# Feed-forward activation transposed by block turns and sixteen small DMAs instead of by TensorE

## The reference

```
for l in range(DEPTH):                      # DEPTH = 2
    ...
    x = x + (mixed @ w_o[l])
    h = rms_norm(x, ffn_norm[l])
    gate, up = split(h @ w_gate_up[l], 2)   # each 256 x 5632
    x = x + ((silu(gate) * up) @ w_down[l])
```

## Time and profile before

| | us |
|---|---|
| median of 3 runs | 2346.24 (2345.91 to 2346.59) |
| the profiled execution | 2346.4 |
| its span, first to last instruction | 2344.1 |
| PE busy | 2320.8 (99%) |
| DVE busy | 1323.1 (56%) |
| ACT busy | 1102.6 (47%) |
| POOL busy | 36.0 (2%) |

### The profile page before, as it was taken

The page is one execution under the profiler, slowest core; times in us unless marked ns, Lnnn a source line. Parts: engine busy times, 40 slices in busy tenths (PEclk is TensorE's granted clock), DMA queues, the critical chain, the costliest instruction groups (busy, mean ns, idle before and its releaser), DMA issues.

```text
span 2344.1 us, 33374 instructions
## 1 busy us (share of the span) xinstructions
PE 2320.8 (99%) x13481; PEld 1922.3 (82%) x13481; DVE 1323.1 (56%) x1420; ACT 1102.6 (47%) x1362; POOL 36.0 (2%) x50
## 2 busy tenths in 40 slices
PE   8999999999999999999999999999999999999999
PEld 7888688888888888888888886888888888888887
DVE  5686676545454445445557857665554444454454
ACT  6554755544443344444445547464444433444433
POOL 0000100000000000000000001000000000000000
PEclk9999999999999999999999999999999999999999
DMA  7453305555555555555554533145555555555553
GB/s 300 166 185 121 131 21 185 189 184 195 187 189 190 190 195 197 182 195 180 194 184 153 196 110 108 39 167 189 184 196 187 189 190 190 195 196 183 194 182 141
DMA packets 59518, 407.03 MB, mean 174 GB/s; under 512 B 6608, under 2 KB 6704, under 8 KB 13200
## 3 DMA queue, kind: packets, MB, share of 16 engines
q1 hardware_dynamic: 58720, 401.66, 48.2%
q0 software_dynamic: 688, 3.78, 0.5%
HBM read 403.32 MB, written 2.10 MB: 173 GB/s over the span
## 4 chain that ended last, share of the span: by engine, by line
PE 95%; DVE 2%; ACT 1%; issue 0%; DMA 0%; SPq 0%; DVEq 0%; ACTq 0%
PE psum L1466 28%; PE psum L1468 28%; PE psum L1467 28%; PE psum L1660 2%; PE psum L1755 2%; PE psum L1909 1%; PE psum L1996 1%; PE psum L1561 1%; PE psum L1500 1%; PE psum L1710 1%; PE psum L1716 0%; DMA x<-x_in_dram 0%; PE psum L1764 0%; PE psum L1569 0%; ACT arena L644 0%
## 5 line engine op out<-in xcount | busy, mean ns | idle before, releaser
L881 DVE TENSOR_TENSOR w_lo<-raw,w_hi 128x1024 fp32r<-128x1024 f32 (+2 forms) x752 | 901.3, 1205 | 844.6 <-ACT w_hi L442 838.1
L442 ACT ACTIVATE w_hi<-raw 128x1024 fp32r<-128x1024 f32 (+2 forms) x752 | 782.0, 1044 | 1071.6 <-PE psum L1468 1070.1
L1466 PE MATMUL psum<-w_hi,hT_hi 128*128 128x512 f32 (+2 forms) x2128 | 821.6, 386 | 3.7 <-DVE w_lo L881 3.7
L1468 PE MATMUL psum<-w_hi,hT_lo 128*128 128x512 f32 (+2 forms) x2128 | 816.5, 384 | 0.0
L1467 PE MATMUL psum<-w_lo,hT_hi 128*128 128x512 f32 (+2 forms) x2128 | 816.3, 384 | 0.0
L1466 PEld LDWEIGHTS psum<-w_hi,hT_hi 128*128 128x128 f32 x2128 | 399.7, 188 | 82.3 <-DVE w_lo L881 2.4
L1468 PEld LDWEIGHTS psum<-w_hi,hT_lo 128*128 128x128 f32 x2128 | 399.6, 188 | 78.2
L1467 PEld LDWEIGHTS psum<-w_lo,hT_hi 128*128 128x128 f32 x2128 | 399.8, 188 | 76.7
L1466 PE MATMUL psum<-w_hi,act_hi 128*128 128x512 f32 x872 | 340.4, 390 | 0.0
L1468 PE MATMUL psum<-w_hi,act_lo 128*128 128x512 f32 x872 | 339.4, 389 | 0.0
L1467 PE MATMUL psum<-w_lo,act_hi 128*128 128x512 f32 x872 | 339.3, 389 | 0.0
(11 more groups left out here) (315 smaller groups left out, 1133.1 us busy)
## 6 DMA issues: line engine op xcount, KB each, us to landing
raw<-stream_dram SPq DMA_DIRECT2D x360, 1024.0 KB, 4.8
raw<-stream_dram SPq DMA_DIRECT2D x16, 512.0 KB, 3.8
raw<-stream_dram SPq DMA_DIRECT2D x8, 768.0 KB, 4.3
raw<-stream_dram SPq DMA_DIRECT2D x8, 640.0 KB, 3.9
x<-x_in_dram SPq DMA_DIRECT2D x4, 512.0 KB, 9.3
lor<-lora_dram POOLq DMA_DIRECT2D x2, 832.0 KB, 10.4
con<-consts_dram POOLq DMA_DIRECT2D x1, 1648.0 KB, 11.2
out_dram<-x SPq DMA_DIRECT2D x3, 512.0 KB, 7.1
```

What stands on the lines that cost most here:

```text
L442: nc.scalar.activation(w_hi[:, q % HALF_RING, 0:2 * w], raw[:, j % 4, hf * 2 * w:(hf + 1) * 2 * w], ACT.Copy).then_inc(hi_done, 1)
L881: tt(w_lo[:, q % HALF_RING, 0:2 * w], raw[:, j % 4, hf * 2 * w:(hf + 1) * 2 * w], w_hi[:, q % HALF_RING, 0:2 * w].bitcast(F32), SUB).then_ ...
L1466: mm(o, a_hi, w_hi[:, r, cols], start=(k == 0), stop=False)
L1468: last = mm(o, a_lo, w_hi[:, r, cols], start=False, stop=(k == n_k - 1))
```

## The change

PE's turn is gone, with its waits. In its place:

- DVE writes act_row so that the two token tiles alternate in runs of 32 columns, and then turns all 32x32 blocks of the 128x1024 tile with one transpose instruction into `act_blocks` (half of `gain`). It waits for the end of that before it goes on.
- A full transpose also needs the blocks moved between the four groups of 32 partitions. POOL waits for each pair's block turn and issues sixteen DMAs of 32 partitions x 256 columns (32 KB), from `act_blocks` to `act_moved` (the other half of `gain`): one for each pair of source and target group, 22 x 16 = 352 in all.
- ACT and DVE read `act_moved` where they read PSUM; ACT waits for all sixteen DMAs.

```
+        act_blocks = gain[:, 0:2 * CH]
+        act_moved = gain[:, 2 * CH:4 * CH]
+        n_moves = (P // 32) ** 2
...
+                for i in range(sum(PAIRS) * l, sum(PAIRS) * (l + 1)):
+                    pool.wait_ge(S("act_blocks_turned"), i + 1)
+                    for q in range(P // 32):
+                        for b in range(P // 32):
+                            pool.dma_start(act_moved[32 * q:32 * q + 32, 256 * b:256 * b + 256],
+                                           act_blocks[32 * b:32 * b + 32, 256 * q:256 * q + 256]).then_inc(
+                                               S("act_moved"), 16)
...
                     def turned_hi(i, p0):
-                        act.wait_ge(S("act_turned"), i + (p0 + 1))
-                        dst = act_hi[:, bass.ds(i * 4, 4), :] if not isinstance(i, int) else act_hi[:, 4 * i:4 * i + 4, :]
-                        nc.scalar.activation(dst, bank(4, 2).rearrange("p (k t) -> p k t", k=4),
+                        act.wait_ge(S("act_moved"), i * (16 * n_moves) + 16 * n_moves * (p0 + 1))
+                        k = bass.ds(i * 4, 4) if not isinstance(i, int) else slice(4 * i, 4 * i + 4)
+                        nc.scalar.activation(act_hi[:, k, :].rearrange("p k (t b e) -> p (k t) b e", t=TT, e=32),
+                                             act_moved.rearrange("p (b n e) -> p n b e", n=8, e=32),
                                              ACT.Copy).then_inc(S("act_hi_ready"), 1)
...
-                        if not isinstance(i, int) or i + p0 > 0:
-                            dve.wait_ge(S("act_turned"), i + p0)
-                        stt(act_row[:, 0, :], psum[:, 2, :], rstd[:, 0:1], silu[:, 0, :], MUL, MUL)
-                        stt(act_row[:, 1, :], psum[:, 3, :], rstd[:, 1:2], silu[:, 1, :], MUL, MUL).then_inc(acc_free[1], 1)
+                        for t in range(TT):
+                            last = stt(act_row.rearrange("p a b -> p (a b)").rearrange(
+                                "p (n t r) -> p t n r", n=16, t=TT)[:, t],
+                                psum[:, 2 + t, :].rearrange("p (n r) -> p n r", n=16), rstd[:, t:t + 1],
+                                silu[:, t, :].rearrange("p (n r) -> p n r", n=16), MUL, MUL)
+                        last.then_inc(acc_free[1], 1)
                         dve.wait_ge(acc_free[1], i + (gate_base + 2))
                         dve.sem_inc(S("act_row_ready"), 1)
+                        nc.vector.transpose(act_blocks.rearrange("p (q k n) -> p k q n", q=4, k=4),
+                                            act_row.rearrange("p a b -> p (a b)").rearrange(
+                                                "p (k q n) -> p k q n", k=4, q=4)).then_inc(
+                            S("act_blocks_turned"), 1)
+                        dve.wait_ge(S("act_blocks_turned"), i + (p0 + 1))
...
-                        tt(act_lo[:, k, :], bank(4, 2).rearrange("p (k t) -> p k t", k=4), act_hi[:, k, :].bitcast(F32),
+                        hi, lo = (z[:, k, :].rearrange("p k (t b e) -> p (k t) b e", t=TT, e=32) for z in (act_hi, act_lo))
+                        tt(lo, act_moved.rearrange("p (b n e) -> p n b e", n=8, e=32), hi.bitcast(F32),
                            SUB).then_inc(S("act_lo_ready"), 1)
...
-                            if u == 0 and not first:
-                                turn(i - 1, pair0)
...
-                            if c == 0 and j == 3:
-                                turn(pairs - 1, pair0)
```

More of the change, by code:

```diff
@@ L1988, in _ @@
                     makes_norm = part == len(PAIRS) - 1 and l < DEPTH - 1
-                    def turn(i, p0):
-                        pe.wait_ge(S("act_row_ready"), i + (p0 + 1))
-                        if not isinstance(i, int) or i + p0 > 0:
-                            pe.wait_ge(S("act_lo_ready"), i + p0)
-                        for k in range(4):
-                            for t in range(TT):
-                                last = tr(bank(4, 2)[:, k * SEQ + t * P:k * SEQ + (t + 1) * P],
-                                          act_row[:, t, k * P:(k + 1) * P], ident)
-                        last.then_inc(S("act_turned"), 1)
                     def pair(i, first):
```

## The result

| us | before | changed kernel |
|---|---|---|
| median | 2346.22 | 2325.01 |
| lowest and highest | 2345.91 to 2346.59 | 2324.94 to 2325.03 |
| profiled execution | 2346.4 | 2325.02 |
| its span | 2344.1 | 2323.2 |

The changed kernel takes 0.9909 of the time of before (95% interval 0.9892 to 0.9927), 21.2 us less. Of the kernel with sixteen idle DMAs at the ends (experiment 2), one execution of ten took 2900.95 us at a granted clock of 0.749 and is left out.

The account below looks back on a forecast made before the run. PE bounds the kernel, on the chain for 95%. From the profiled 2346.4 us, 22 turns take off 19.5 and the rest adds 0, giving 2326.9; the median stands 0.2 below, 2326.7 us. Range 2325 to 2346.

Parts of the forecast that it names:

- the gain per turn: PE in the feed-forward layers: each turn of eight transposes costs 0.887 us on the path, 22 turns 19.5 us.
- Nothing else leaves PE: PE: beyond the 22 turns, 19.5 us, no other PE time is saved.
- that is all that can be gained: Below the forecast time, only a 1% error in the 0.887 us per turn could bring more gain.
- The allowance below: Lower edge of the range, 2325 us, for the 0.887 us perhaps being 1% off.
- DVE's work: DVE: one added block turn of 128x1024, 1.246 us, delays the next w_lo by 1.3 us, hidden by some 5.8 us.
- The chain: Block turn's end to act_hi: sixteen POOL issues 0.53 us apart, 8.0 us, landing 4.3 us; 12.4 us in all.
- The deadline at a part's end: Four part ends: data needed by 2249.2, landing at 2248.7, so 0.5 us in hand.
- Four microseconds for each beyond: Part ends: each microsecond of landing beyond 4.8 us costs 4 us, one at each of four ends.
- Inside the loop: Pairs not ending a part: data may land 24.1 us after the block turn, so the move is free.
- Rival 1: Small DMAs land late behind weight packets: 2339.5 us at 8 us, 2356 at 12.2; in part 0.15, far end within 0.16.
- Rival 2: DVE's w_lo holds up POOL's issues: chain 19.0 us, kernel 2351 us; turning point 17.7 us; within a shared 0.16.
- POOL's other work: POOL's three loads for layer 1 leave after layer 0's last pair, land within 7 us or so; first reader 1331.8.

Follow-up runs that it names:

- experiment 2: Changed kernel with sixteen more small idle DMAs ahead of the real ones for the last pair of each part: 2350.3 us, ratio 1.0016.
- the doubled turns: Kernel before, with each of PE's 22 turns made twice in a row: 2366.09 us against 2345.96.
- The padding: 67 semaphore increments that nobody waits for, put into PE's program of layer 0: changed kernel 2325.55 us; kernel before 2347.2 us against 2346.02.
- the pair of kernels with one PE program: Changed kernel with nine norm turns also moved to DVE and POOL, 2327.02 us, and that with 16 idle DMAs more per layer, 2326.14 us.
- additions: Changed kernel with four DVE additions of 128x512 tiles behind the block turn at each part's end: 2325.63 us.
- 48 idle DMAs: Changed kernel with 48 idle DMAs issued by GpSimd ahead of the first pair of each layer: 2327.33 us.
- copies: Changed kernel with six DVE float32 copies of 128x512, SBUF to SBUF, behind the block turn at each part's end: 2331.3 us.
- norms: Changed kernel with three of four column chunks of norms 1 to 3 also turned by DVE and POOL, not PE: 2327.02 us.
- norms and 16 idle: The kernel that also turns the norms by blocks, with 16 idle DMAs ahead of the first norm's in each layer: 2326.14 us.
- eight idle DMAs: Changed kernel with eight idle DMAs ahead of the real ones for the last pair of each part: 2340.53 us.
- twice the DMAs: Changed kernel with sixteen idle DMAs ahead of the real ones for the 18 pairs that are not the last of a part: 2325.05 us.

## Why the prediction was right, and where it was wrong

**What bounds the kernel, and the gain per turn:** right. PE's rows from start to start gave 0.887 us, the trace of after and the doubled turns 0.905 and 0.88. That term was 0.4 us short in the sum.

**The steps that failed: "Nothing else leaves PE" and "that is all that can be gained".** The prediction took removed work for the whole of what a shorter program can do, and put everything else that PE might lose or gain at nothing. The runs showed 0.94 us more: PE's own pause in layer 1, which was there before and is not there in the changed kernel. With the pause still there the time would be about 2326, in the range; without it, it is 2325.01, at the edge. The other step is the size of a turn, 0.887 us in the sum and 0.905 measured, 0.4 us in all. The allowance below was too small by its own reason, too: 1% of 0.887 is 0.2 us in all, and the measured price was 2% higher. The padding shows that the pause depends on the instructions ahead, and the pair of kernels with one PE program that it depends on more than those. So this part of the gain is luck, and no property of moving the turns. A range should have let the time fall by such a pause as well as rise by it: 1 us below, or to 2324.

**DVE's work** at no cost: right. The block turn takes 1.25 us as read from the earlier trace rows.

**The chain:** right in its order, 1.2 us long at the last end. The issues come 0.49 us apart, not the 0.53 of the earlier trace rows, which makes 0.6 us less, and the last lands 3.5 us after its issue starts, not 4.3.

**The deadline at a part's end:** this was the best number. Forecast were 12.9 us from the end of the block turn. Over the experiments, the idle time of PE follows the chain less 13.0:

| kernel, end | chain | PE idle in its row | lost per end |
|---|---|---|---|
| changed kernel, last | 11.2 | 0 | 0 |
| additions, last | 13.1 | 0 | 0 |
| 48 idle DMAs, part 0 | 14.0 | 0.88 | 1.1 |
| copies, last | 14.2 | 1.16 | |
| norms, part 0 of layer 0 | 14.9 | 1.78 | 2.1 |
| norms and 16 idle, part 0 of layer 0 | 15.2 | 2.10 | |
| copies, part 1 of layer 0 | 15.6 | 2.74 | |
| norms, part 0 of layer 1 | 15.8 | 2.66 | 3.0 |
| eight idle DMAs, last | 16.0 | 2.94 | 4.5 (mean of four) |
| norms and 16 idle, part 0 of layer 1 | 16.3 | 3.15 | |
| sixteen idle DMAs, last | 17.3 | 4.24 | 6.3 (mean of four) |

So 1.8 us were in hand where the prediction had 0.5. "Four microseconds for each beyond" holds for the rows in which the granted clock stays at 1.00. In both kernels with idle DMAs at the ends it falls to 0.50 behind the hole, and each end costs 1.5 to 2 us more; it falls as well behind the longer hole of the copies and behind both of the last kernel. Rivals 1 and 2 were priced without this: their turning point, a chain of 17.7 us, is in truth between 16.0 and 17.3.

**Inside the loop:** free, as forecast, also with twice the DMAs.

**Rival 1** did not occur in the changed kernel, but its cause is real: around the issue of a weight load landings run to 5.3 us there, and to 7.8 with copies, against 1.7 away from one.

**Rival 2:** no stretched issues under w_lo, and under copies only the first, by 0.23 us. The late landings with copies come from a weight load that stands later and is slow.

**POOL's other work:** right. The loads for layer 1 now start at 1068.63 and their first reader on DVE comes at 1321.8.

**What the prediction did not see at all** is POOL's pause of 3.4 us in each layer. It fell on pair 8, where 24 us are forgiven. On a part's end it costs 2 to 3 us, as in the kernel with the norms. That none of the four ends has it is luck, not a property of the change.

## What to carry to other kernels

A transpose on a saturated PE is worth its distance from start to start, here 0.11 us for 128x128, and can be given to DVE's block turn and a handful of small DMAs wherever the consumer can wait some 11 us; find the one or two places where it cannot, reckon the deadline back from the first late consumer, and keep 2 us in hand. What puts off a weight load can move it onto the last of the small DMAs. A late chain costs its lateness and, in some executions, a stretch at half clock behind the hole as well. When a program gets shorter or longer, allow one or two microseconds either way for pauses that move.

## What the runs showed of the hardware that I had not expected

- PE pauses for no semaphore in the middle of a group of small matmuls, by 0, 0.34, 0.6, 1.5, 1.7 or 1.8 us. Instructions far ahead of it change that, and two kernels with the same PE program have 1.8 and 0. PE goes on 2.2 to 2.5 us after a 16 KB packet of an instruction queue has started.
- GpSimd pauses likewise: its first issue comes 3.38 us after the block turn and not 0.29, before the 129th of its 32 KB DMAs in a layer, after having waited 35 us for a semaphore and not during that wait. Idle DMAs between the pairs moved that place, idle DMAs at the start of the layer did not.
- Small DMAs from GpSimd land 1.7 to 2.2 us after their issue starts away from the issue of a weight load, and 3 to 8 us around it.
- Work on VectorE that touches neither the tile nor the queue lengthens a chain of DMAs by 1.4 to 2.0 us (additions) or 1.5 to 4.6 us (copies), and the rows of the issues don't show it: it moves a weight load by 2.5 us, onto the last of them.
- Behind a hole without matmuls the granted clock can go from 1.00 to 0.50, for 2 to 5 us of matmuls. With eight idle DMAs it did so at all four ends, even behind the one with 2.06 us of idle in its row, and with the norms and 16 idle DMAs behind 2.10; in the kernel with the norms it stayed at 1.00 behind 1.78 and 2.66 us. So the length of the hole alone does not say whether the clock falls, and what does was not tried.
